# FFN first halves with the weights stationary: high weights move 512 columns, low weights 256, and two engines add the halves of a PSUM bank

## The reference, cut to what matters

```python
def swiglu(x, w_in, w_out):            # w_in 1024 x 5632, w_out 2816 x 1024
    gate, up = jnp.split(x @ w_in, 2, axis=-1)
    return (jax.nn.silu(gate) * up) @ w_out
...
h = h + 0.5 * rms_norm(swiglu(rms_norm(h, g[0]), ffn_w_in[i, 0], ffn_w_out[i, 0]), g[1])
...
gate, up = jnp.split(h2 @ w_ffn_in[l], 2, axis=-1)
x = x + g2[:, None, :] * ((jax.nn.silu(gate) * up) @ w_ffn_out[l])
```

## Time and profile before

| | |
|---|---|
| median of 3 runs | 2811.11 us (2810.86 to 2811.58) |
| span of the profiled execution, first to last instruction | 2808.9 us |
| TensorE matmul busy | 2777.8 us, 99% of the span, 13354 matmuls |
| VectorE, ScalarE, GpSimd busy | 66%, 55%, 7% |
| granted TensorE clock, mean | 0.999 |
| DMA | 559 MB, 199 GB/s |

### The profile page before, as it was taken

The page is one execution under the profiler, slowest core; times in us unless marked ns, Lnnn a source line. Parts: engine busy times, 40 slices in busy tenths (PEclk is TensorE's granted clock), DMA queues, the critical chain, the costliest instruction groups (busy, mean ns, idle before and its releaser), DMA issues.

```text
span 2808.9 us, 34710 instructions
## 1 busy us (share of the span) xinstructions
PE 2777.8 (99%) x13354; PEld 2268.2 (81%) x13354; DVE 1855.1 (66%) x2704; ACT 1538.8 (55%) x2662; POOL 186.7 (7%) x300
## 2 busy tenths in 40 slices
PE   8999999999999999999999999999999999999998
PEld 7888788888888888886888888788788788788787
DVE  6766776676667667667676776667754755745754
ACT  6547754654665465467654645765454544444543
POOL 1000100000000010015001001110000000000000
PEclk9999999999999999999999999999999999999999
DMA  7765467566536756651666675367665565654652
GB/s 260 236 210 190 143 211 254 188 225 225 187 126 213 254 188 212 238 205 54 195 225 226 216 249 207 110 216 234 213 218 195 187 203 190 211 194 165 208 182 105
DMA packets 358660, 559.40 MB, mean 199 GB/s; under 512 B 15680, under 2 KB 245056, under 8 KB 358240
## 3 DMA queue, kind: packets, MB, share of 16 engines
q1 hardware_dynamic: 350752, 535.02, 56.4%
q0 software_dynamic: 7600, 21.81, 2.3%
q10 hardware_dynamic: 144, 0.36, 0.0%
HBM read 556.03 MB, written 1.10 MB: 198 GB/s over the span
## 4 chain that ended last, share of the span: by engine, by line
PE 95%; DVE 2%; ACT 1%; issue 1%; DMA 0%; POOL 0%; SPq 0%; DVEq 0%; ACTq 0%
PE ps L703 40%; PE ps L793 27%; PE ps L709 20%; PE ps L673 4%; PE ps L874 1%; PE ps L905 1%; ACT SB L1593 1%; PE ps L762 1%; ACT JUNK L1441 0%; PE ps L915 0%; PE ps L882 0%; DVE M L2005 0%; DMA RAW<-in_ffn_w_in 0%; PE ps L850 0%; PE ps L1053 0%
## 5 line engine op out<-in xcount | busy, mean ns | idle before, releaser
L703 PE MATMUL ps<-HI,XH 128*128 128x512 f32 x2480 | 983.3, 396 | 3.2 <-DVE LO L1865 2.4
L703 PE MATMUL ps<-LO,XH 128*128 128x512 f32 x2480 | 967.9, 390 | 0.0
L1860 DVE TENSOR_TENSOR LO<-RAW,HI 128x1024 fp32r<-128x1024 f32 x468 | 568.8, 1223 | 342.4 <-ACT HI L1421 338.3
L709 PE MATMUL ps<-HI,XL 128*128 128x512 f32 x2480 | 767.6, 391 | 0.4
L1865 DVE SCALAR_TENSOR_TENSOR LO<-RAW,GC,HI 128x512 fp32r<-128x512 f32 (+1 forms) x896 | 623.5, 746 | 189.1 <-ACT HI L1428 186.7
L1421 ACT ACTIVATE HI<-RAW 128x1024 fp32r<-128x1024 f32 x468 | 492.4, 1059 | 450.5 <-PE ps L793 296.0
L1428 ACT ACTIVATE HI<-RAW,GC 128x512 fp32r<-128x512 f32 (+1 forms) x896 | 587.7, 714 | 152.2 <-PE ps L709 126.9
L709 PEld LDWEIGHTS ps<-HI,XL 128*128 128x128 f32 x2480 | 463.6, 188 | 107.8 <-DVE XL L1901 9.7
L703 PEld LDWEIGHTS ps<-HI,XH 128*128 128x128 f32 x2480 | 466.0, 188 | 100.7 <-DVE LO L1865 3.6
L703 PEld LDWEIGHTS ps<-LO,XH 128*128 128x128 f32 x2480 | 466.1, 188 | 92.0
L793 PE MATMUL ps<-HI,AH 128*128 128x512 f32 x856 | 266.3, 392 | 0.0
(11 more groups left out here) (221 smaller groups left out, 2085.6 us busy)
## 6 DMA issues: line engine op xcount, KB each, us to landing
RAW<-in_ffn_w_in SPq DMA_DIRECT2D x350, 512.0 KB, 4.6
RAW<-in_ffn_w_out SPq DMA_DIRECT2D x88, 1024.0 KB, 4.9
RAW<-in_w_ada SPq DMA_DIRECT2D x48, 1024.0 KB, 5.0
RAW<-in_w_in SPq DMA_DIRECT2D x44, 1024.0 KB, 5.0
RAW<-in_w_ffn_in SPq DMA_DIRECT2D x88, 512.0 KB, 4.6
RAW<-in_diff_w_in SPq DMA_DIRECT2D x24, 1024.0 KB, 5.0
RAW<-in_w_ffn_out SPq DMA_DIRECT2D x22, 1024.0 KB, 4.9
RAW<-in_moba_w_in SPq DMA_DIRECT2D x12, 1024.0 KB, 5.0
```

Of the source, the lines that this page charges most:

```text
L703: e.matmul(ps[:, b + t, 0:nw], XH[:, k, t * P:(t + 1) * P], q[s][:, c * nw:(c + 1) * nw], start=(k == 0 and q is HI), stop=False)
L709: i = e.matmul(ps[:, b + t, 0:nw], XL[:, k, t * P:(t + 1) * P], HI[s][:, c * nw:(c + 1) * nw], start=False, stop=(k == 7))
L1860: e.tensor_tensor(LO[n % NSPLIT][:, 0:w], RAW[t.buf][:, at[1] * w:(at[1] + 1) * w], HI[n % NSPLIT][:, 0:w].bitcast(F32), ALU.subtract).the ...
```

## The change

In blocks 1 to 10 of every FFN first half the roles change. XH and XL become one tile XHL in which each chunk has its 256 high and 256 low columns side by side. A quarter of a block's columns (128 gate or up columns) is stationary. With the high weights the 512 columns of XHL move, with the low weights the 256 of XH, so a split takes 8 matmuls of 512 and 8 of 256 columns, into four banks (0 to 3 and 4 to 7 in turn). The result has features on partitions; a bank's first half holds high x high, its second half the two other terms. ScalarE copies the four second halves to T, VectorE adds gate, then up. There is no transpose but of block 0, which stays as it was. As tokens are now columns, the root is a row: two transposes turn it once in a step ("ffn" only), ScalarE copies it to RB, and VectorE multiplies the gate by it. The up half isn't multiplied any more; instead the 1e-6 of the norm behind is multiplied by the mean square (`eps_of`, two more operations on GpSimd in a step, and a wait on VectorE in `by_gain`). AH and AL are made from AF in SBUF. Waits: a block waits for AF of the block before last, as before; chunk k of the second half waits for AL of block k // 2. The last AH comes behind one more split on ScalarE.

```diff
...
         HI = [sb(f"HI{i}", [P, HW], F32R) for i in range(NSPLIT)]
         LO = [sb(f"LO{i}", [P, HW], F32R) for i in range(NSPLIT)]
-        XH = sb("XH", [P, KC, S], F32R)
-        XL = sb("XL", [P, KC, S], F32R)
+        XHL = sb("XHL", [P, KC, 2, S], F32R)
+        XH, XL = XHL[:, :, 0, :], XHL[:, :, 1, :]
         stage_at = place["sb"]
         place["sb"] = STAGE_END
         RAW = [sb(f"RAW{i}", [P, TW]) for i in range(NRAW)]
...
+                x["RB"] = stage_sb(f"RB{k}", [P, S])
+                x["T"] = stage_sb(f"T{k}", [P, 4, S])
...
         def part(x, h):
             return x[:, h * 512:(h + 1) * 512]
+        def eps_of(st, t):
+            c = 96 + 2 * (st.k % 2) + t
+            return ST[:, c:c + 1], st.c["ep"] + t + 1
         def root_of(st, t):
...
                 AH, AL, AF, ACC = (st.t[x] for x in ("AH", "AL", "AF", "ACC"))
                 c = st.c
-                def activations_turned(jp, b):
-                    e.wait_ge(s_af, c["af"] + jp + 1)
-                    if jp >= 1:
-                        e.wait_ge(s_al, c["al"] + jp)
-                    turn(ps[:, b, :], [AF[:, jp % 2, t, j * P:(j + 1) * P] for j in range(2) for t in range(2)]
+                def first_turned():
+                    e.wait_ge(s_af, c["af"] + 1)
+                    turn(ps[:, 0, :], [AF[:, 0, t, j * P:(j + 1) * P] for j in range(2) for t in range(2)]
                          ).then_inc(s_tf, 1)
+                def roots_turned():
+                    for t in range(2):
+                        r, n = root_of(st, t)
+                        e.wait_ge(s_pw, n)
+                        i = e.transpose(ps[:, 1, t * P:(t + 1) * P], r.to_broadcast([P, P]), ident)
+                    i.then_inc(s_rbt, 1)
+                def features_by(n, k2, b):
+                    s = n % NSPLIT
+                    quarters = [(c, gu, j) for c in range(2) for gu in range(2) for j in range(2)]
+                    for c, gu, j in quarters:
+                        e.matmul(ps[:, b + 2 * gu + j, :], HI[s][:, c * 512 + gu * S + j * P:][:, 0:P],
+                                 XHL[:, 2 * k2 + c].rearrange("p a n -> p (a n)"), start=(k2 + c == 0), stop=False,
+                                 skip_group_check=True)
+                    for c, gu, j in quarters:
+                        i = e.matmul(ps[:, b + 2 * gu + j, S:2 * S], LO[s][:, c * 512 + gu * S + j * P:][:, 0:P],
+                                     XH[:, 2 * k2 + c, :], start=False, stop=(2 * k2 + c == 7), skip_group_check=True)
+                    return i
                 first_block(st, 512)
                 for jp in range(1, JP):
-                    b = 2 * ((jp + 1) % 2)
+                    b = 4 * (jp % 2)
                     if jp >= 2:
                         e.wait_ge(s_af, c["af"] + jp - 1)
+                    if jp == 2:
+                        e.wait_ge(s_al, c["al"] + 1)
+                        if st.fold:
+                            e.wait_ge(s_rb, c["rb"] + 1)
                     for k2 in range(4):
-                        if k2 == 2:
-                            activations_turned(jp - 1, 4)
+                        if jp == 1 and k2 == 2:
+                            if st.fold:
+                                roots_turned()
+                            first_turned()
                         n = st.w0 + 4 * jp + k2
                         taken(n)
-                        for t in range(2):
-                            i = tokens_by(n, k2, t, b, 512, None, None)
-                        i.then_inc(s_used, 1)
+                        features_by(n, k2, b).then_inc(s_used, 1)
                 def ready(k, t):
                     if (k, t) == (0, 0):
-                        e.wait_ge(s_al, c["al"] + JP - 1)
-                    elif (k, t) == (FC - 2, 0):
-                        e.wait_ge(s_al, c["al"] + JP)
+                        e.wait_ge(s_af, c["af"] + JP - 1)
+                    if t == 0 and k % 2 == 0:
+                        e.wait_ge(s_al, c["al"] + k // 2 + 1)
                 def hook(k, t):
-                    if (k, t) == (0, 1):
-                        activations_turned(JP - 1, 2)
                     last_hook(st, k, t, FC)
                     if t == 1 and k == ADA_SUMS and st.ada:
                         e.wait_ge(s_ada, c["ada"] + 24)
-                        e.wait_ge(s_af, c["af"] + JP - 1)
+                        e.wait_ge(s_af, c["af"] + JP)
                         for q in range(3):
                             i = e.matmul(ps[32 * q:32 * q + 1, 0, :], ONE[:, 0:1], ACC[:, q, :], start=True, stop=True)
...
             def ffn(st):
                 c = st.c
-                AH, SG = st.t["AH"], st.t["SG"]
+                AH, SG, AF, RB, T = (st.t[x] for x in ("AH", "SG", "AF", "RB", "T"))
                 second_rows(st)
-                def activations_high(jp, b):
-                    e.wait_ge(s_tf, c["tf"] + jp + 1)
-                    e.activation(AH[:, 2 * jp:2 * jp + 2, :], ps[:, b, :].rearrange("p (j n) -> p j n", j=2), ACT.Copy
-                                 ).then_inc(s_ah, 1)
+                def activations_high(jp):
+                    if jp == 0:
+                        e.wait_ge(s_tf, c["tf"] + 1)
+                        src = ps[:, 0, :].rearrange("p (j n) -> p j n", j=2)
+                    else:
+                        e.wait_ge(s_af, c["af"] + jp + 1)
+                        src = AF[:, jp % 2]
+                    e.activation(AH[:, 2 * jp:2 * jp + 2, :], src, ACT.Copy).then_inc(s_ah, 1)
                 for jp in range(JP):
-                    b, i = 2 * ((jp + 1) % 2), jp % 2
+                    i = jp % 2
                     if jp >= 1:
                         split(st.w0 + 4 * jp + 7)
                         if jp == 1 and st.k == 0:
                             e.wait_ge(s_c, 16)
                             e.activation(CS[:, :], CS[:, :], ACT.Silu).then_inc(s_cs, 1)
-                        activations_high(jp - 1, 4)
+                        if jp == 1 and st.fold:
+                            e.wait_ge(s_rbt, c["rbt"] + 1)
+                            e.activation(RB[:, :], ps[:, 1, 0:S], ACT.Copy).then_inc(s_rb, 1)
+                        activations_high(jp - 1)
                         split(st.w0 + 4 * jp + 9)
-                    e.wait_ge(s_used, st.w0 + 4 * jp + 4)
-                    if jp >= 2:
-                        e.wait_ge(s_af, c["af"] + jp - 1)
+                    if jp >= 1:
+                        e.wait_ge(s_used, st.w0 + 4 * jp + 4)
+                        if jp >= 2:
+                            e.wait_ge(s_up, c["up"] + jp - 1)
+                        e.activation(T[:, :, :], ps[:, 4 * i:4 * i + 4, S:2 * S], ACT.Copy).then_inc(s_t, 1)
+                        e.wait_ge(s_gr, c["gr"] + jp)
+                        e.activation(SG[:, i], SG[:, i], ACT.Silu).then_inc(s_sg, 1)
+                        continue
+                    e.wait_ge(s_used, st.w0 + 4)
                     if st.fold:
                         for t in range(2):
                             r, n = root_of(st, t)
                             e.wait_ge(s_pw, n)
-                            o = e.activation(SG[:, i, t], ps[:, b + t, 0:S], ACT.Silu, scale=r)
+                            o = e.activation(SG[:, 0, t], ps[:, 2 + t, 0:S], ACT.Silu, scale=r)
                         o.then_inc(s_sg, 1)
                     else:
-                        e.activation(SG[:, i], ps[:, b:b + 2, 0:S], ACT.Silu).then_inc(s_sg, 1)
-                activations_high(JP - 1, 2)
+                        e.activation(SG[:, 0], ps[:, 2:4, 0:S], ACT.Silu).then_inc(s_sg, 1)
+                split(st.w0 + 4 * JP + 6)
+                activations_high(JP - 1)
                 split(st.w1 + 2)
             def copy_out(st, n, dst, b, nw, func=ACT.Copy):
...
             def by_gain(b, t):
                 s0, s1, v = stats_of(b.k, t)[:3]
+                eps = 1e-6
+                if steps[b.k - 1].kind == "ffn":
+                    eps, n = eps_of(steps[b.k - 1], t)
+                    e.wait_ge(s_ep, n)
                 e.wait_ge(s_g[b.g1.buf], 16 * b.g1.turn)
                 if by_halves(steps[b.k - 1]):
                     for h in range(2):
                         e.wait_ge(s_sq, b.f_sq[t] + h + 1)
                         if h == 1:
-                            e.tensor_scalar(v, s0, s1, 1e-6, ALU.add, ALU.add).then_inc(s_v, 1)
+                            e.tensor_scalar(v, s0, s1, eps, ALU.add, ALU.add).then_inc(s_v, 1)
                         e.scalar_tensor_tensor(out=part(M[:, t, :], h), in0=ps[:, 4 + 2 * t + h, :], scalar=b.coef,
                                                in1=part(G[b.g1.buf], h), op0=ALU.mult, op1=ALU.mult).then_inc(s_y, 1)
                     return
...
             def ffn(st):
                 c = st.c
-                AH, AL, SG, AF, ROW = (st.t[x] for x in ("AH", "AL", "SG", "AF", "ROW"))
```

(61 more changed lines are left out.)

## The result

The changed kernel takes 2793.58 us (median of 4 runs, 2793.48 to 2793.91) against 2811.07 of the kernel before (2810.86 to 2811.58): a ratio of 0.9937, 95% interval 0.9923 to 0.9951. It is faster by 17.5 us, about half of the 34.2 forecast, and 1.6 us above the range. The direction was right, the size wrong. The worst case that the prediction had worked out, 2796, still holds it; the range left out its last 4 us.

The account below looks back on a forecast made before the run. TensorE, busy 99% of the span, was taken to bound the kernel. Terms -48.5 + 12.2 + 1.8 + 0.3 = -34.2 us gave a span of 2774.7 and a forecast of 2776.9 us, range 2764 to 2792.

Parts of the forecast that it names:

- The worst case that the prediction had worked out, 2796: Whole kernel with every term at its worst: 2776.9 + 13.8 + 4.5 + 1.3 = 2796 us.
- The bound: Whole kernel: TensorE, busy 99% of the span, sets the time; other engines cost nothing until they make it wait.
- The sets, -48.5: FFN first halves: transpose sets that go, 90 at 0.49 us and 10 at 0.44; bounds 44.0 and 49.0.
- The matmuls that change, +12.2: Blocks 1 to 10: 3200 narrow matmuls (256 columns) at 117.2 ns, each 3.8 ns above half a wide one.
- its upper bound of 26: Changed matmuls at worst: 15.7 us for narrow ones 118.3 ns apart, 10.4 for 13 ns at each of 800 width changes.
- Root and boundary, +1.8 and +0.3: Two more root transposes in each of eight steps, +1.8 us; mean square's 1e-6 from a column, 16 times, +0.3 us.
- VectorE and ScalarE at nothing: Changed blocks: their added work costs nothing, hidden behind a new block of 11.01 us on TensorE.
- The walked loop, 10.1 us: VectorE's order from one gate add to the next in a changed block: 10.1 us, 0.9 less than a block.
- 1 (the pace of VectorE): Changed blocks: VectorE and ScalarE set the pace; +16 us, 2793, or +12, 2789; chance 10%.
- 2: Narrow matmuls: weight load not hidden; wholly exposed +333 us, 3098; 20 ns exposed gives 2829; chance 7%.
- 3: Transpose sets: their 0.49 us comes back as a wait for LO, time within 0.2%; chance 5%.

Follow-up runs that it names:

- the kernel of only narrow ones: Changed kernel with each wide matmul (512 columns) split into two of 256 with a load each; 2828.79 us, ratio 1.006.
- the run without narrow ones: Changed kernel with the 3200 narrow matmuls (256 columns) left out, so part of the product is missing; 2587.56 us, ratio 0.9204.
- the additional operation: Changed kernel with one more VectorE multiplication of 1024 columns, into a tile nobody reads, at the end of each changed block; 2792.79 us, ratio 0.9934.
- Strict alternation: Changed kernel with each narrow matmul (256 columns) issued directly behind its wide one (512 columns); 2791.03 us, ratio 0.9927.

## Why the prediction was right in direction and wrong in size

- **The bound** was read rightly: TensorE sets the time before and after, and every microsecond is one of its stream.
- **The sets, -48.5:** held as far as tested. Doubling them gave 0.40 of work each, the wide ones behind a set show 0.06 of disturbance, and the sum below closes to 0.7 us with 0.49. (The 24 matmuls in 5.44 us that priced a wide one are two splits, not four as the prediction says; the price is right.)
- **The matmuls that change, +12.2:** this is the step that failed. Shown is 11.17/4 = 2.792 us a split against 2.722, 400 x 70.5 ns = +28.2. The term was mis-sized by 16 us, and its upper bound of 26 was too low as well. Two things are in it. A narrow matmul costs 120.0 and not 117.2, 9 us: 18 scattered distances in another step were taken for a steady price. Half a wide one (113.4) holds only half of the 13.3 ns that the kernel of only narrow ones showed, and a narrow one bears them whole: 113.4 + 6.7 = 120. And a run of narrow ones makes the wide ones behind it slow for five matmuls, net 20 ns a split, 8 us. The forecast had nothing for this. Its bound had 13 ns at each of 800 changes, 10.4 us, which covers it; the bound failed at the narrow ones, 15.7 us where 3200 x 6.6 = 21 were due. The rows behind the earlier trace rows showed the disturbance to its end; timeline of the kernel before:

```profile
1251.38 0.40 PE L703 MATMUL ps<-HI,XH 128*128 128x512 f32 x1
...
1252.08 0.40 PE L703 MATMUL ps<-LO,XH 128*128 128x512 f32 x1
1252.31 0.62 PE L709 MATMUL ps<-HI,XL 128*128 128x512 f32 x2
1252.77 0.39 PE L703 MATMUL ps<-HI,XH 128*128 128x512 f32 x1
```

  Six wide ones take 1252.77 - 1251.38 = 1.39 us, 30 ns more than 6 x 226.7.
- **Root and boundary, +1.8 and +0.3:** the root as forecast, 0.22 for each of eight; the boundary wasn't tried by itself.
- **VectorE and ScalarE at nothing:** right. The walked loop, 10.1 us, was 0.85 too long by the run without narrow ones, on the safe side.
- **The sum** with the measured term: -48.5 + 28.2 + 1.8 + 0.3 = -18.2; measured -17.5.
- **Rivals:** 1 (the pace of VectorE) did not occur, as the additional operation shows. 2 did not occur in its form, but its subject was the right one: the narrow matmul costs more than its columns. 3 did not occur.

## What to carry to other kernels

An exchange of operand roles that keeps the columns is still priced by the number of matmuls: here 13.3 ns for each one more, each with its load of 128 columns, and 20 ns for each return from a run of short ones to long ones. Take a unit price from a steady stretch of the same form, and read a disturbance to its end and not only its first distance. Where short and long instructions must be mixed in runs, longer runs cost less, as far as the buffers carry them (11.11 us a block with 32 of each, 11.17 with 8). Strict alternation cost as little in its good pattern (32 x 346.7 = 11.09 us), but it did not hold that pattern everywhere.

## What had not been expected

Wide matmuls stay 1 to 9 ns slower for five behind narrow ones, and somewhat slower for six to ten behind a wait of TensorE, though 227 ns leave ample room for a weight load (a load with 128 moving columns takes 112 in all); what makes this is not shown. In strict alternation two steady patterns exist, 347 and 353 ns a pair, and what chooses between them is open. A block with all four splits held to its end loses time only behind block 1 (0.71 us), where the wait is for AL of block 0 and not for a split. And in the run without narrow ones a wait of 4.3 us was followed by 4.3 us at half the granted clock, in which the 13.3 ns of a matmul don't show.
